# Samples of the down products summed apart, and VectorE's side work put at other units, in a decoder trunk on one core

## The reference, cut to what matters

```
mix = concat(o_gla, o_lru, o_mla) @ w_out
x = LN(ALPHA * x + gate1 * mix)
h2 = x * (1 + scale2) + shift2
g_ff, u_ff = split(h2 @ ffn_w_gu)             # 1024 -> 2 x 2816
f = (silu(g_ff) * u_ff) @ ffn_w_down          # 2816 -> 1024
x = LN(ALPHA * x + gate2 * f)
```

## Time and profile before

| what | value |
|---|---|
| median of 3 runs (lowest, highest) | 3627.26 us (3620.04, 3630.15) |
| the profiled execution, its span | 3621.66 us, 3619.9 us |
| TensorE matmuls | 3291.5 us busy (91%) |
| TensorE weight loads | 2765.7 us busy (76%) |
| VectorE | 2348.2 us (65%) |
| ScalarE | 1579.6 us (44%) |
| mean granted clock of TensorE | 0.951 |
| feed-forward stage, first layer (products and down parts) | from about 1000 to about 1792 us, then part 15 and the last norms |
| the same, second layer | from about 2782 to about 3577 us, then part 15 and the end |

### The profile page before, as it was taken

How to read it: one execution, slowest core, us unless ns; L and a number is a source line. 1 busy time by engine, 2 the same in 40 slices (tenths; PEclk the granted TensorE clock), 3 DMA queues, 4 the chain that set the end, 5 groups by cost and what they waited for, 6 DMA issues and landing times. The chain is left out here.

```text
span 3619.9 us, 61473 instructions
## 1 busy us (share of the span) xinstructions
PE 3291.5 (91%) x23676; PEld 2765.7 (76%) x23676; DVE 2348.2 (65%) x4510; ACT 1579.6 (44%) x3163; POOL 193.8 (5%) x252
## 2 busy tenths in 40 slices
PE   6988898998999998999979868989989899999997
PEld 5864556776988888999869535666769898899996
DVE  5135665445488889878742366644446888888887
ACT  5235454444254454444332445544433454543432
POOL 0011210110000000000000121111100000000000
PEclk9997999998999999999989969999999999999998
DMA  5144002443033232222111500034411233322231
GB/s 209 32 142 155 26 1 94 163 153 104 13 110 93 88 95 79 85 81 84 48 52 30 194 29 1 1 142 159 167 47 58 82 99 89 91 82 79 88 105 52
DMA packets 157573, 316.91 MB, mean 88 GB/s; under 512 B 18491, under 2 KB 85341, under 8 KB 146406
## 3 DMA queue, kind: packets, MB, share of 16 engines
q1 hardware_dynamic: 145766, 229.08, 20.4%
q0 software_dynamic: 11520, 83.89, 6.5%
HBM read 306.41 MB, written 6.51 MB: 86 GB/s over the span
## 5 line engine op out<-in xcount | busy, mean ns | idle before, releaser
L2383 ACT CAST w_ffn_hi<-w_ffn 128x512 fp32r<-128x512 f32 x616 | 366.8, 617 | 283.8 <-DVE w_ffn L2562 192.9
L437 PE MATMUL psum<-h_lo,w_ffn_hi 128*128 128x256 f32 (+1 forms) x1408 | 407.6, 290 | 0.0
L436 PE MATMUL psum<-ffn_act_hi,w_down_hi 128*128 128x288 f32 (+1 forms) x992 | 341.5, 344 | 63.9 <-DVE w_down_lo L2580 56.7
L2574 DVE TENSOR_TENSOR w_ffn_lo<-w_ffn,w_ffn_hi 128x1024 fp32r<-128x1024 f32 (+1 forms) x366 | 383.9, 1049 | 15.6 <-ACT w_ffn_hi L2383 15.3
L436 PE MATMUL psum<-h_forms_hi,w_ffn_hi 128*128 128x288 f32 x1232 | 365.1, 296 | 3.9 <-DVE w_ffn_lo L2574 3.4
L436 PE MATMUL psum<-h_hi,w_ffn_hi 128*128 128x256 f32 x1232 | 348.7, 283 | 18.9 <-DVE w_ffn_lo L2574 17.1
L438 PE MATMUL psum<-h_forms_hi,w_ffn_lo 128*128 128x288 f32 x1232 | 364.3, 296 | 0.0
L438 PE MATMUL psum<-h_hi,w_ffn_lo 128*128 128x256 f32 x1232 | 347.1, 282 | 0.0
L438 PE MATMUL psum<-ffn_act_hi,w_down_lo 128*128 128x288 f32 (+1 forms) x992 | 333.4, 336 | 0.0
L437 PE MATMUL psum<-ffn_act_lo,w_down_hi 128*128 128x288 f32 (+1 forms) x992 | 333.2, 336 | 0.0
L422 DVE SCALAR_TENSOR_TENSOR xT<-psum,adaT,xT 128x512 f32<-128x512 f32 (+3 forms) x432 | 235.0, 568 | 142.2 <-PE psum L438 142.0
(11 more groups left out here) (443 smaller groups left out, 7608.8 us busy)
## 6 DMA issues: line engine op xcount, KB each, us to landing
w_ffn<-in_w_gu SPq DMA_DIRECT2D x352, 256.0 KB, 2.6
w_ada_pair<-in_w_ada SPq DMA_DIRECT2D x40, 1024.0 KB, 5.2
w_down<-in_w_down SPq DMA_DIRECT2D x192, 192.0 KB, 2.4
w_ada_first<-in_w_ada SPq DMA_DIRECT2D x4, 2048.0 KB, 21.7
w_out<-in_w_out SPq DMA_DIRECT2D x16, 512.0 KB, 7.4
w_in_T<-in_w_in_T SPq DMA_DIRECT2D x12, 512.0 KB, 4.4
w_down<-in_w_down SPq DMA_DIRECT2D x48, 128.0 KB, 2.1
z<-in_x_prompt SPq DMA_DIRECT2D x8, 512.0 KB, 6.9
```

The source lines that it names most:

```text
L436: pe.matmul(o, wh, xh, start=first, stop=False)
L437: pe.matmul(o, wh, xl, start=False, stop=False)
L2383: act.copy(WGH[:, (j + 1) % NR].bitcast(F32R), WGR[:, m % 2, i]).then_inc(s_wh, 1)
L2574: dve.tensor_tensor(WGL[:, m % 2, i:i + n].bitcast(F32R), WGR[:, m % 2, i:i + n], WGH[:, r:r + n], ALU.subtract).then_inc(s_wl, n)
```

## The change

- Units (`down_units`) of parts 8 to 14 start with both halves of blocks 0 and 1, where they had the first halves of blocks 0 to 3. So the wait for the second half of the activations moves from the fifth unit to the third.
- The sample columns of parts 8 to 14 are no longer gated and added to `XT` unit by unit: `residual_summed` adds them ungated from PSUM to `SACC` (blocks 0 to 6) or to `TMPF[:, 1]` (block 7), one instruction instead of two with a wait; part 8 copies instead. `samples_added` gates and adds all of it after part 14, with two instructions of 448 columns and two of 64.
- VectorE's side work in a down part (`beside`) is put at units given by `BESIDE`. First half: rests at units 2, 3, 4 as before; statistics at 3 (was 1), their second step at 5 (was 4, ahead of the last rest), sums at 4 (was 3). Second half: rests at 5, 7, 8 (was 7, 9, 11), statistics at 3 (was 5), second step at 9 (as before), sums at 10 (was 6), rests for the next part at 11, 13, 15 as before.
- On ScalarE the roots and the first `norm1` or `norm2` come after the last `down_rounded`, where they stood ahead of it.
- The sums are made in the order 1, 3, 2, 4, so that the piece rounded second waits for two sums instead of three; in the products two are made at step 1 and two at step 2, after the rests.
- `mod1` and `mod2` are issued one at a time, at steps 1 to 4 of two pairs.

```diff
-            def modulate(eng, par, g, t0, t1):
+            def modulate(eng, par, g, t0, t1, one=None):
...
-                for k in range(par, KD, 2):
+                for k in range(par, KD, 2) if one is None else (par + 2 * one,):
...
-                return [(u % 4 if u < KD else u // 2, HALVES[1][u // 4 if u < KD else u % 2], 4 + u % 4)
-                        for u in range(2 * KD)]
+                first = [(0, 0), (1, 0), (0, 1), (1, 1)] + [(u // 2, u % 2) for u in range(4, 2 * KD)]
+                return [(c, HALVES[1][h], 4 + u % 4) for u, (c, h) in enumerate(first)]
...
+        BESIDE = [((2, 3, 4), 3, 5, 4, (5, 6, 7)), ((5, 7, 8), 3, 9, 10, (11, 13, 15))]
...
                         for u in range(first):
+                            if u == 2:
+                                pe.wait_ge(s_ul, 2 * m1)
                             part(u, last).then_inc(s_dn, 1)
...
-                            if u == first:
-                                pe.wait_ge(s_ul, 2 * m1)
                             part(u, last).then_inc(s_dn, 1)
...
-                            act.wait_ge(s_ws, 4 * m + {3: 1, 2: 2, 1: 3, 6: 4}[i])
+                            act.wait_ge(s_ws, 4 * m + {3: 1, 1: 2, 2: 3, 6: 4}[i])
...
-                        if m == PAIRS[QH - 1][0] and i in (1, 4):
-                            mod1(act, i // 4, 2, TB0, TP)
-                        if not final and m == PAIRS[QH + 6][0] and i in (1, 4):
-                            mod2(act, i // 4, 0, 0, 512)
+                        r = 4 * (m - PAIRS[QH - 1][0]) + i - 1
+                        if PAIRS[QH - 1][0] <= m < PAIRS[QH - 1][0] + 2 and 1 <= i <= 4:
+                            mod1(act, r // 4, 2, TB0, TP, r % 4)
+                        r = 4 * (m - PAIRS[QH + 6][0]) + i - 1
+                        if not final and PAIRS[QH + 6][0] <= m < PAIRS[QH + 6][0] + 2 and 1 <= i <= 4:
+                            mod2(act, r // 4, 0, 0, 512, r % 4)
...
                         for c in range(NW, KD if q < NQ - 1 else NW):
-                            if c == KD - 1:
-                                norms_beside(q, 1)
                             down_rounded(q, c)
                             if q == QH - 1:
                                 form_rounded(1, c - 2)
+                        norms_beside(q, 1)
                         norms_beside(q, 2)
...
-                        if i == 2 and m + 1 < NPAIR and not (m == m0 and q - 1 in SUMS_IN_D):
-                            for n in range(1, 5):
-                                w_sum(m + 1, n)
                         for g in LO_AT[j]:
                             w_rest(*g)
+                        if i in (1, 2) and m + 1 < NPAIR and not (m == m0 and q - 1 in SUMS_IN_D):
+                            for n in ((1, 3), (2, 4))[i - 1]:
+                                w_sum(m + 1, n)
...
+                    def beside(q, u, b):
+                        for c in range(NW, KD):
+                            if u == b[0][c - NW]:
+                                down_rest(q, c)
+                        if u == b[1]:
+                            norms_beside(q, True)
+                        if u == b[2]:
+                            norms_beside(q, False)
+                        if u == b[3] and q in SUMS_IN_D:
+                            for n in (1, 3, 2, 4):
+                                w_sum(PAIRS[q][1] + 1, n)
+                        if u in b[4]:
+                            for g in LO_D[q][b[4].index(u):b[4].index(u) + 1]:
+                                w_rest(*g)
+
+                    def sample_sum(c):
+                        return SACC[:, c] if c < KD - 1 else TMPF[:, 1]
+
+                    def residual_summed(q, ps, c, span):
+                        t0, w = span
+                        wp = TP - t0
+                        dve.scalar_tensor_tensor(XT[:, c, t0:TP], ps[:, 0:wp], ADA[:, M_G2 + c, 0:1], XT[:, c, t0:TP],
+                                                 ALU.mult, ALU.add)
+                        if q == QH:
+                            dve.wait_ge(s_ev, 3 * KD)
+                            ins = dve.tensor_copy(sample_sum(c), ps[:, wp:w])
+                        else:
+                            ins = dve.tensor_tensor(sample_sum(c), ps[:, wp:w], sample_sum(c), ALU.add)
+                        ins.then_inc(s_dv, 1)
+
+                    def samples_added():
+                        dve.wait_ge(s_dv, U0[NQ - 1])
+                        for c0, c1, v in ((0, KD - 1, SACC), (KD - 1, KD, TMPF[:, 1:2])):
+                            v4 = v.rearrange("p c (b t) -> p c b t", b=SB)
+                            lk2(dve.tensor_tensor(v4, v4, bc(ADA[:, M_G2 + c0:M_G2 + c1, 1:9], ST), ALU.mult))
+                            lk2(dve.tensor_tensor(XT[:, c0:c1, TP:T], XT[:, c0:c1, TP:T], v, ALU.add))
...
-                            residual(dve, lk2, s_dv, TMPF, bank(b), c, span, M_G2)
-                            if q < NQ - 1 and u + 1 == DONE[q][c]:
-                                norms_beside(q, c)
-                                late = int(q >= QH)
-                                if 2 + late <= c <= 4 + late:
-                                    down_rest(q, c + 3 - late)
-                                if c == 3 - late and q in SUMS_IN_D:
-                                    for n in range(1, 5):
-                                        w_sum(PAIRS[q][1] + 1, n)
-                                if c >= 5:
-                                    for g in LO_D[q][c - 5:c - 4]:
-                                        w_rest(*g)
+                            if QH <= q < NQ - 1 and span[0] + span[1] > TP:
+                                residual_summed(q, bank(b), c, span)
+                            else:
+                                residual(dve, lk2, s_dv, TMPF, bank(b), c, span, M_G2)
+                            if q < NQ - 1:
+                                beside(q, u, BESIDE[q >= QH])
...
                         down(q)
+                        if q == NQ - 2:
+                            samples_added()
```

More of the change, by code:

```diff
@@ L2074, in build @@
         P1T, U3T, C22T, U2T = (UTS[:, i] for i in range(4))
-        assert o + 5 * 1152 <= r1
+        SACC = at("down_samples", o + 4 * 1152, [P, KD - 1, TS])
+        assert o + 4 * 1152 + (KD - 1) * TS * 4 <= r1
         ZF = at("ln2_rows", r1, [P, 5, 2, 512])
@@ L2563, in w_sum @@
                         if p == 4:
-                            dve.wait_ge(s_ws, 4 * m + 3)
+                            dve.wait_ge(s_ws, 4 * m + 2)
                             ins = dve.tensor_tensor(w[:, 6], w[:, 4], w[:, 1], ALU.subtract)
@@ L2605, in up_gated, with norms_beside @@
                                           ALU.mult).then_inc(s_um, 1)
-                    def norms_beside(q, c):
-                        if c == 1:
+                    def norms_beside(q, first):
+                        if first:
                             for blk in LN1_AT.get(q, ()):
@@ L2612, in norms_beside @@
                                 stats2(dve, lk2, blk)
-                        if c == 4:
+                        else:
                             for blk in LN1_AT.get(q, ()):
@@ L2752, in _ @@
                         if u == 13:
-                            for p in range(1, 5):
+                            for p in (1, 3, 2, 4):
                                 w_sum(0, p)
```

## The result

The changed kernel takes a median of 3570.18 us (4 runs, 3566.56 to 3571.51), against 3628.68 us (4 runs, 3620.04 to 3630.15) for the kernel before beside it: ratio 0.9842, interval 0.9825 to 0.9860. A second comparison, in a later set of runs, gave 3568.24 us against 3623.53 and 0.9858 (0.9835 to 0.9881). The profiled execution took 3571.02 us, its span is 3569.2 us, against 3621.66 and 3619.9.

A forecast was written before the change was run, and what follows sets the result against it. TensorE's matmuls fill 91% of the span; the order of VectorE's work makes it wait. Gains 34.3 + 11.6 + 13.1 = 59.0 us from 3621.66 give 3562.7; the median, 5.6 above, gives 3568, stated as 3567 (own range 3555 to 3582).

The forecast's parts named there:

- The down-weight waits and the clock with them: TensorE's waits for down-weight rests fall from 57 us to under 10; parts 9 to 13 run at clock 1.00.
- Second half: Down parts 8 to 14: gain 17.2 us in the first layer and 17.1 in the second, together 34.3.
- The wait at unit 15 of parts 8 to 11: Last layer: TensorE waits some 0.85 us for bank 7, as VectorE still has residual 11 to do.
- the bounds 0 and 1.1: Parts 8 to 14: loss per part to late activations at the third unit, 0 to 1.1 us; 0 and 0.4 taken.
- First half, down parts: Down parts 0 to 7: gain 6.1 and 5.5 us in the two layers, together 11.6.
- The new wait: Part 0: norms start about 1050.5, TensorE idles 3.8 us for them and goes on at 1052.9.
- Products: Products of the up weights: gain 6.8 and 6.3 us in the two layers, sum 13.1, ends 0 and 20.5.
- Rival 2: Clock falls at new waits, parts 0 and 1 and last layer's second half: 10 x 1.7 = 17 us, 3584; chance 0.10.
- Rival 1: 28 part ends lose 0.7 us each to late activations, products win nothing: 30 us gained, 3597; chance 0.22.
- Rival 3: All of TensorE's waits go, in both layers: 80 us gained, 3547; chance 0.12.
- Rival 4: Sums at step 1 of the products wait for weight transfers; 58 us would cancel the gain: slower, 3640; chance 0.03.
- `samples_added`: Ahead of part 15's products: about 2 us of VectorE once a layer, covered; without that cover, 4 us.

The follow-up runs named there:

- the order alone: Changed kernel with the samples gated and added unit by unit as before, all else changed: 3572.06 us, ratio 0.9875.
- the lighter sample work alone: Kernel before with only `residual_summed` and `samples_added`, order and units as before: 3605.07 us, ratio 0.9962.
- the kernel without that wait: Changed kernel with the norms' second step at unit 4 in the first half and the sums at unit 11 in the second: 3545.12 us, ratio 0.9789.
- the kernel with the old sums: Changed kernel with the four sums in order 1, 2, 3, 4, all at step 2 ahead of the rests: 3578.63 us, ratio 0.9884.
- the norm kernel: Changed kernel with the norms' second step in the first half at unit 4 instead of 5, ahead of the sums: 3551.19 us, ratio 0.9811.
- the kernel with the old units: Changed kernel with `down_units` and the place of the wait for `s_ul` as before: 3572.19 us, ratio 0.9870.

## Why the prediction came out as it did

*The down-weight waits and the clock with them* went as predicted: 56.7 to 6.3 us, what stays is part 7's, the clock of parts 9 to 13 is 1.00, and their lengths are 20.6 to 21.2 us in the first layer, 20.6 to 21.8 in the second. The other signs came too: waits for rests of up weights 10.0 us (7 to 12), L426 and L429 32 times each, and waits for activations 1.6 and 3.5 us a layer, where over 10 would have been against it. That the order of the work was the cause and not VectorE's amount of it is shown by the two kernels with half of the change each: the order alone takes the waits away (6.5 us left), the lighter sample work alone leaves 52.0. Of the order, the runs took back the order of units, the place of the sums in the products and the modulation one by one, and none of them brings these waits back. What is left is the side work's places on VectorE in the down parts and the casts ahead of the norms on ScalarE; no run parts these two. In part 0 before, VectorE stood 1.40 us for a cast that ScalarE made only after its first norm, so both may have a share.

*Second half.* First layer 16.7 for 17.2. Second layer 14.3 for 17.1, and that term is mis-sized in four places. The wait at unit 15 of parts 8 to 11 was sized right:

```profile
3245.44 0.37 PE L436 MATMUL psum<-ffn_act_hi,w_down_hi 128*128 128x288 f32 x1 [0.85 <-DVE down_samples L2708]
```

but parts 9 to 11 gain 2.5, 2.8 and 2.5 where 3.0 each was put down: 3.0 leaves 24.30 - 3.0 - 0.85 = 20.45 us for TensorE's own work, and the kernel without that wait takes 20.71, so this was 0.3 too low, and 0.2 more than the 0.85 went with the wait. Parts 12 and 13 gain 1.1 and 0.8 where 1.2 each was, for they got the activation waits that were given the bounds 0 and 1.1, and the value taken, 0.4, was too low there:

```profile
3394.48 0.40 PE L436 MATMUL psum<-ffn_act_hi,w_down_hi 128*128 128x288 f32 x1 [0.39 <-DVE ffn_act_lo L2595]
...
3396.11 0.41 PE L436 MATMUL psum<-ffn_act_hi,w_down_hi 128*128 128x288 f32 x1 [0.57 <-DVE ffn_act_lo L2595]
```

0.96 in part 12, 1.10 in part 13. Part 14 gained 2.3 of 2.7, with 1.30 us of waiting for bank 7 (the second profile of this kernel has 0.82 there, and the part is 0.6 shorter, so this one may be scatter). Part 8 has a wait that the prediction did not name, for the transposes of layer norm, which need the bank that VectorE's last addition of the products empties: 1.27 us in the first layer (0.85 before), 0.92 in the second (none before). It gained 1.8 and 2.2 us where 2.2 and 3.0 were put down.

```profile
1415.93 1.09 PE L310 MATMUL psum<-consts,xT 128*128 128x128 f32 x8 [1.27 <-DVE ffn_u L2657]
```

*First half, down parts.* 12.0 for 11.6, partly by offsetting errors. The new wait came as put down: norms from 1050.52 (predicted 1050.5), TensorE on at 1052.87 (1052.9), idle 3.45 us (3.8), since TensorE was done at 1049.4 and not at 1049.1. Part 0 gained 1.5 and 1.6 for 0.6, since the clock's share of it moved into the products behind; parts 4, 5 and 6 gained 1.9 or 1.2, 1.7 and 1.7 (2.0 or 1.3, 1.7, 1.7); parts 2 and 3 together gained 1.0 in each layer for 0.4. Part 7, put at 0, lost 1.1 and 2.1. 0.9 of either are its waits for the activations (0.63, new) and for a residual (1.79 for 1.52 and 1.75 for 1.51). In the second layer most of the rest is the clock: before, it fell in the products of part 8, at 3180.1 us, and now in part 7, at 3126.0; the second profile of the changed kernel, in which it does not fall there, has part 7 at 22.57 us instead of 23.42. (The prediction's terms for the second layer add up to 5.4, not 5.5.)

*Products.* 8.2 for 13.1, the largest error. The sums' new place was sized a little low in part 3 (1.2 for 0.8 to 0.9), part 7 too high (2.1 for 2.7), and part 0 far too high: 1.0 was put down and 0.2 came, in both layers. But the products of parts 1 and 2, where +0.8 and 0 were put down, lost 0.4 and 1.6 in each layer, 4.0 us together, because the clock fell after every one of the four long norm waits. (The kernel with the norms' second step ahead has these products at 30.50 and 30.92 us in the first layer, where this one has 32.02 and 31.53.) Two things went the other way and hid a part of it: the products of part 8 in the second layer, where the clock fell before and not now, gained 2.3 for 1.0, and those of parts 9, 11 and 13, where nothing was put down, 0.3 each. The step that failed is the one that says of the clock in part 0 that it would cost what it cost before, "only earlier", and of part 1 that it "may now fall": in part 1 it did, in both layers. Rival 2 had charged exactly this, 1.7 us four times; of its other six places, the short waits in the second layer, none came about: the waits of 0.85 us in parts 8 to 11 and of 1.30 in part 14 left the clock at 1.00, as nearly all waits of that length did (last section).

*Rival 1*, VectorE giving the gain back at the activations, came about in part 7, in part 14 and in parts 12 and 13 of the second layer alone: 5.1 us of such waits in the two stretches, where it had 20. *Rival 3*, all waits gone for 80 us, had against it that VectorE has no room in the first half. That reason holds for part 7, whose waits stay, but not for parts 0 to 6: with one number of `BESIDE` changed the norm waits go, and with two the sum of parts is 78.5 us below the kernel before. *Rival 4:* the up weights land in 2.4, 2.6, 5.3 us (min, median, max; before 2.3, 2.6, 5.3), and ScalarE waited 2.1 us for them in all; the sums at step 1 waited for none:

```profile
  ACT w_ffn_hi L2385: 2.1, 2
...
DMA to landing us min/median/max: 2.4/2.6/5.3
```

*`samples_added`* stayed out of sight, as costed: part 15's products take 22.36 and 22.37 us where they took 22.37 in both layers. The modulations, singly, are worth the 0.9 us twice in part 7, not 2.7; the rest of part 7's 2.1 is the sums, 1.2 by the kernel with the old sums.

*The number.* The forecast of 3567 is 3 us from the median, though its sum was 8 us too large: 59.0 for 51.1. The execution profiled before was 5.6 us under the median that the prediction knew (7.0 under that of the four runs), and this one is 0.8 above its own. So the medians are 58.5 us apart, 55.3 in the second comparison, and the two profiled executions 50.6. That 3567 came so near is in part luck of the executions; what the sum got wrong is read from the parts, of which the clock behind the norms is clear of the scatter, as the norm kernel shows.

The cost left over is shown too. With the norms' second step one unit earlier, 20.9 us go; with the second half's sums one unit later as well, 23.1, beside the changed kernel of the second set. Four sums and a residual, 1046.94 to 1050.1, stand ahead of a step of 0.6 us (1050.13 to 1050.76) on which ScalarE, and through it TensorE, waits. That order is not new. The kernel before had it too, in part 0 of the first layer:

```profile
1046.69 0.69 DVE L2565 TENSOR_TENSOR w_ffn<-w_ffn 128x512 f32<-128x512 f32 x1
1047.30 0.75 DVE L422 SCALAR_TENSOR_TENSOR xT<-psum,adaT,xT 128x512 f32<-128x512 f32 x1
1047.96 0.15 DVE L337 RECIPROCAL ln_rstd<-ln_std 128x1 f32<-128x1 f32 x1
...
1049.98 0.56 DVE L2580 TENSOR_TENSOR w_down_lo<-w_down,w_down_hi 128x384 fp32r<-128x384 f32 x1 [1.40 <-ACT w_down_hi L2388]
```

There its price stood under another name. The last cast of down weights came behind the first norm, VectorE waited 1.40 us for it, and TensorE for the rest until 1050.60; both norms were done at 1051.1, before TensorE asked for their banks at 1054.17. The change took that chain away but moved the step 2 us later in the part (from 17.8 to 19.8 us after its start), and so laid the norm's own wait bare.

## What to carry to other kernels

Where an engine in strict order serves several waiters, what matters is which pieces stand ahead of the one that TensorE waits for, not the engine's busy share: putting the short step that another engine waits for (the norm's second step) ahead of the long work that nobody waits for yet (the sums) was worth 21 us, more than a third of what the whole change brought. When a change takes away the longest wait, look for what it had hidden: the same four sums stood ahead of that step before, when the waits were put down to a rest of weights. Count the whole chain behind each new wait, and where, in a kernel like this one, the wait may be 2 us or more, add the clock (1.5 us here). Savings on the same resource don't add: 1.8 us less of VectorE's work per part was worth 15.9 us by the sums of parts while the order was bad, mostly by the clock, and 2.5 us after.

## What the runs showed of the hardware that was not expected

Which waits of TensorE are followed by a fall of its clock. Over the ten traces of this case, in the feed-forward stretches (before: from 1000 to 1792 us and from 2782 us on; the others: from 1000 to 1765 us and from 2755 us on), each wait of TensorE was held against the stretches in which the granted clock is 0.50. Of 24 waits of 3.4 us, 23 have such a stretch, of 44 waits from 2.0 to 2.5 us, 28, of 205 waits from 0.8 to 1.95 us, 2 (one of 1.92 in the kernel before and the one of 1.52 above). It begins from 0.4 us before the wait's end to 1.9 us behind it. The last wait of each trace, 8.6 us and followed by transposes, is not counted. Each stretch lasts 3.4 us at 0.50, the 1.2 GHz level, and costs about 1.5 us where like work can be compared: in the kernel with the old units the products of part 2 take 31.56 us with one in the first layer and 30.01 without one in the second. Where VectorE is the limit it costs less: part 7 and the products of part 8 take 58.6 us together in the first layer in both profiles of the changed kernel, with the stretch in the first and without it in the second.

The Trainium skill ("TensorE: Matmul & The Clock Gate", HAM oscillation) has waits between bursts bring the clock down each time. The waits of its example are about 3 to 5 us. For the waits of 3.4 us the traces agree (23 of 24). From 2.0 to 2.5 us it is a chance of two in three, and below that there is nearly no case. The same wait in the same place of the same kernel goes either way: 2.19 us in part 7 of the first layer brought the clock down in the first profile of the changed kernel, and 2.17 us there did not in the second.
